# Eight projections of a two-block fp32 kernel computed as seven quarter products instead of eight

## The reference, cut to what matters

```python
# first block, x is (256, 1024)
yf = jnp.square(jax.nn.relu(hf @ w_up[l])) @ w_down[l]        # w_down (4096, 1024)
x = x + rmsnorm(yf, g_norm[l, 5])
# second block, h is (272, 1024): 16 meta tokens ahead of x
    return (y * g) @ w_o, v_first                             # time mixing, w_o (1024, 1024)
    return (jax.nn.silu(gate) * val) @ w_down                 # both FFNs, (2816, 1024)
            if layer == N_A:
                kvn = rms_norm(h, kv_norm_g)
                k_sh = to_padded_heads(kvn @ sb_wk)
                v_sh = to_padded_heads(kvn @ sb_wv)
            q = to_padded_heads(hn @ sb_wq[j])
            mix_out = stick_breaking_attention(q, k_sh, v_sh) @ sb_wo[j]
        h = h + mix_out
        h = h + conv_glu_ffn(rms_norm(h, norm_ffn_g[layer]), ffn_up[layer], ffn_conv_w[layer],
                             ffn_conv_b[layer], ffn_down[layer])
```

## Time and profile before

| | |
|---|---|
| median of 3 runs | 1638.88 us (1638.53 to 1639.74) |
| the profiled execution | 1636.88 us, of which its span is 1634.8 us |
| PE busy | 1536.2 us, 94% of the span |
| PEld busy | 1290.2 us, 79% |
| DVE busy | 527.2 us, 32% |
| ACT busy | 343.8 us, 21% |
| HBM read | 187.45 MB, 115 GB/s over the span |

### The profile page before, as it was taken

One profiled execution on the slowest core, in us unless ns is written; L12 is line 12 of the kernel. 1 busy time (PEld: TensorE's weight loads), 2 busy tenths in 40 slices (PEclk: granted clock), 3 DMA queues, 4 the chain that ended last, 5 costly groups with the idle time before them and its releaser, 6 DMA issues.

```text
span 1634.8 us, 25810 instructions
## 1 busy us (share of the span) xinstructions
PE 1536.2 (94%) x10548; PEld 1290.2 (79%) x10548; DVE 527.2 (32%) x977; ACT 343.8 (21%) x613; POOL 30.3 (2%) x47
## 2 busy tenths in 40 slices
PE   8999999989999879998888999999998879999997
PEld 6888788988888758577774888888886768888886
DVE  2140233331100273547535244431112542444301
ACT  1231103231100112200111223310102652323101
POOL 0130000000000000000000000000001100000000
PEclk9999999999999999899997999999999669999999
DMA  8444243354444304130000444444443003444441
GB/s 333 143 129 154 77 143 115 132 185 154 150 146 154 115 26 129 52 104 4 4 3 0 142 142 142 144 151 155 149 147 116 0 0 116 143 143 148 144 155 52
DMA packets 54435, 189.75 MB, mean 116 GB/s; under 512 B 6961, under 2 KB 9137, under 8 KB 53970
## 3 DMA queue, kind: packets, MB, share of 16 engines
q1 hardware_dynamic: 50480, 180.67, 33.3%
q10 hardware_dynamic: 3874, 7.85, 1.5%
HBM read 187.45 MB, written 1.05 MB: 115 GB/s over the span
## 4 chain that ended last, share of the span: by engine, by line
PE 89%; DVE 6%; issue 3%; ACT 1%; DMA 0%; POOL 0%; DVEq 0%; ACTq 0%; SPq 0%; PEldq 0%; POOLq 0%
PE ps L1365 88%; DVE arena L1165 1%; DVE arena L1193 0%; DVE arena L1302 0%; DMA ring<-in_stream 0%; DVE rs L1829 0%; DVE arena L1306 0%; DVE arena L1192 0%; DVE arena L1007 0%; DVE arena L999 0%; DVE res L1838 0%; DVE arena L997 0%; DVE arena L1846 0%; DVE arena L1315 0%; ACT L1648 0%
## 5 line engine op out<-in xcount | busy, mean ns | idle before, releaser
L1365 PE MATMUL ps<-arena,ring 128*128 128x272 f32 (+2 forms) x5504 | 1212.1, 383 | 19.7 <-DMA ring<-in_stream 8.2
L1365 PEld LDWEIGHTS ps<-arena,ring 128*128 128x128 f32 x5504 | 1028.3, 192 | 201.9 <-issue 16.0
L1365 PE MATMUL ps<-arena 64*64 64x64 f32 (+7 forms) x3828 | 177.8, 246 | 46.0 <-DVE arena L1315 12.2
L1365 PEld LDWEIGHTS ps<-arena 64*64 64x64 f32 (+3 forms) x3828 | 142.1, 141 | 80.8 <-issue 42.0
L1365 PE MATMUL ps<-arena,consts 128*128 128x16 f32 (+7 forms) x438 | 116.3, 425 | 19.9 <-DVE arena L1306 6.0
L1365 PEld LDWEIGHTS ps<-arena,consts 128*128 128x128 f32 (+3 forms) x438 | 84.8, 234 | 47.3 <-DVE arena L1306 6.1
L910 ACT ACTIVATE arena<-arena,cols 128x272 f32<-128x272 f32 x88 | 53.7, 613 | 184.5 <-DVE arena L1130 184.3
L1137 DVE SCALAR_TENSOR_TENSOR arena<-arena,cols 128x271 f32<-128x271 f32 (+1 forms) x176 | 84.1, 498 | 15.1 <-ACT arena L910 3.2
L1130 DVE TENSOR_TENSOR arena<-ps,rs 128x272 f32<-128x272 f32 x88 | 38.9, 442 | 149.5 <-PE ps L1365 147.7
L1079 DVE TENSOR_TENSOR res<-res,ps 128x272 f32<-128x272 f32 x32 | 14.0, 439 | 194.6 <-PE ps L1365 194.6
L891 ACT ACTIVATE arena<-res 128x272 f32<-128x272 f32 x32 | 13.8, 430 | 212.2 <-DVE res L1079 212.2
(11 more groups left out here) (219 smaller groups left out, 692.1 us busy)
## 6 DMA issues: line engine op xcount, KB each, us to landing
ring<-in_stream SPq DMA_DIRECT2D x342, 512.0 KB, 3.2
consts<-in_consts ACTq DMA_DIRECT2D x1, 1516.0 KB, 8.5
arena<-in_x_t ACTq DMA_DIRECT2D x1, 1024.0 KB, 5.8
arena<-in_mem_t ACTq DMA_DIRECT2D x1, 1024.0 KB, 4.8
res<-in_x_t ACTq DMA_DIRECT2D x1, 1024.0 KB, 14.2
out_t<-arena SPq DMA_DIRECT2D x4, 256.0 KB, 3.0
arena<-in_g ACTq DMA_DIRECT2D x1, 640.0 KB, 5.6
arena<-in_w ACTq DMA_DIRECT2D x2, 256.0 KB, 4.8
```

The lines of the kernel that those rows point to most:

```text
L1365: return nc.tensor.matmul(out, lhs, rhs, start=start, stop=stop)
```

## The change

Two neighbouring output tiles and two neighbouring input tiles make a 256x256 piece of the weights, cut in four quarters a11, a12, a21, a22; the tokens are cut in two halves (t = 128 of 256, or T2 = 136 of 272). The 2x2 product of quarters, which takes eight products of half width, is made from seven (Winograd's form of Strassen's algorithm), each with accumulation over the input tiles in PSUM:

- DVE makes four sums of the weight quarters (`weight_sums`, four instructions 128x512 for each pair of blocks, into one of two buffers) and four sums of the activations' quarters (`x_sums`).
- PE multiplies in the order 1, 6, 7, 4, 5, 2, 3 (`seven_products`); products 6, 7 and 3 and half of the operands come from the sums.
- ACT copies product 1 out of PSUM (`keep_first_product`), since an instruction then reads only one PSUM operand; DVE puts the seven products together into two output tiles (`quads_to_y`, `quads_to_res`, `quads_scaled`).

A pair of output tiles now has 28 matmuls for each group of four pairs of input tiles (21 for the last group of an FFN's down, which has three), where it had 64 wide ones per four blocks. `down` has 4 pairs of 4 groups; `ffa_down` and `ffb_down` 4 pairs of 3 groups (4, 4, 3); the square ones a single group per pair, with the first pair of tiles of `rw_o`, `sb_k` and `sb_o` left as it was. The PSUM banks of even and odd pairs alternate (0 to 3, 4 to 7), and PE starts pair i when the results of pair i - 2 have been taken. The activations' sums of the three down projections are made inside the loops of the up projections. SP's loads of the down projections come in pairs of blocks that belong together. Some one-use semaphores were merged (`arms_pe`, `arms_dve`) to free numbers.

```diff
+        ORDER = (1, 6, 7, 4, 5, 2, 3)
+        SPLIT = {1: (0, 0), 6: (0, 1), 7: (1, 0), 4: (1, 1), 5: (2, 0), 2: (2, 1), 3: (3, 0)}
+        WIDE = {7: (0, 0), 5: (0, 1), 4: (1, 0), 3: (1, 1), 1: (2, 0), 6: (2, 1), 2: (2, 2)}
...
+        def seven_products(pe, mm, name, second=None):
+            y = SEVEN[name]
...
+            x_of = {1: b11, 2: b21, 3: b22, 4: t4, 5: t1, 6: t2, 7: t3}
+            for i in range(y.i0, y.n):
+                if i >= 2:
+                    pe.wait_ge(ev[name], y.off + 2 * (i - 1))
+                if second and i == y.i0 + 1:
+                    second()
+                for g, n in enumerate(y.groups):
...
+                    w_of = {1: a11, 2: a12, 3: s4, 4: a22, 5: s1, 6: s2, 7: s3}
+                    arrived(pe, b)
+                    arrived(pe, b + 1)
...
+                    for p in ORDER:
+                        if p in (6, 7, 3):
+                            pe.wait_ge(w_summed, done + {6: 2, 7: 3, 3: 4}[p])
+                        for l in range(n):
+                            last = mm(product_at(y, i, p), w_of[p][:, l, :], x_of[p][:, 4 * g + l, :],
...
+                        if g == len(y.groups) - 1 and p in (6, 4, 2):
+                            last.then_inc(products, 1)
+                    last.then_inc(used, 2)
+
+        def weight_sums(dve, tt, name, i, g):
...
+            if b - 4 >= y.block(y.i0) or not y.own:
+                dve.wait_ge(used, b - 2)
+            tt(s1, a21, a22, ALU.add).then_inc(w_summed, 1)
+            dve.wait_ge(w_summed, done + 1)
+            tt(s2, s1, a11, ALU.subtract).then_inc(w_summed, 1)
+            tt(s3, a11, a21, ALU.subtract).then_inc(w_summed, 1)
+            dve.wait_ge(w_summed, done + 2)
+            tt(s4, a12, s2, ALU.subtract).then_inc(w_summed, 1)
+
+        def x_sums(link, tt, name, at=slice(None)):
...
+            link(tt(t1, b12, b11, ALU.subtract))
+            link(tt(t2, b22, t1, ALU.subtract))
+            tt(t3, b22, b12, ALU.subtract)
+            tt(t4, b21, t2, ALU.subtract).then_inc(x_summed, 1)
+
+        def seven_vector(dve, tt, name, quads, then=None):
...
+            for at, (_, i, g) in enumerate(work):
+                if at + 1 < len(work):
+                    weight_sums(dve, tt, *work[at + 1])
+                if g == 0 and at and at < len(work) - bool(then):
+                    quads(i - 1)
+            quads(y.n - 1)
...
-            tiles("rw_o", FIRST["rw_o"], 8, bb, L, norm=gated_slice)
+            tiles("rw_o", FIRST["rw_o"], 2, bb, L, norm=gated_slice)
+            seven_products(pe, mm, "rw_o")
...
+            def quads_to_res(name, i, which, queries=False):
...
+                dve.wait_ge(p1_kept, y.pair(i) + 1)
+                tt(u2, p1, pr(6), ALU.add)
+                link(tt(o[0], o[0], p1, ALU.add))
+                dve.wait_ge(products, 3 * y.pair(i) + 2)
+                tt(u3, u2, pr(7), ALU.add)
+                tt(o[1], o[1], u2, ALU.add)
+                link(tt(e[0], e[0], pr(4), ALU.add))
+                tt(e[0], e[0], u3, ALU.add)
+                link(tt(e[1], e[1], u3, ALU.add))
+                dve.wait_ge(products, 3 * y.pair(i) + 3)
+                tt(e[1], e[1], pr(5), ALU.add).then_inc(ev[name], 1)
+                link(tt(o[1], o[1], pr(5), ALU.add))
+                tt(o[0], o[0], pr(2), ALU.add)
+                if i:
+                    link(add_squares(2 * i))
+                dve.wait_ge(used, y.block(i + 1))
+                tt(o[1], o[1], pr(3), ALU.add).then_inc(ev[name], 1)
...
+            def quads_scaled(name, i, dst):
...
+                dve.wait_ge(used, y.block(i + 1))
+                dve.wait_ge(p1_kept, y.pair(i) + 1)
+                link(tt(u2, p1, product_at(y, i, 6), ALU.add))
+                tt(quarters[:, 2, :], p1, product_at(y, i, 2), ALU.add)
+                link(tt(uv, two(7), over(u2, 2), ALU.add))
+                tt(quarters[:, 0:4:3, :], uv, two(4), ALU.add)
+                link(tt(quarters[:, 1, :], uv[:, 0, :], product_at(y, i, 5), ALU.add))
+                part = dst[:, 2 * i:2 * i + 2, :]
+                tt(part, part, over(rs[:, 0:L], 2), ALU.mult).then_inc(ev[name], 2)
...
-            take_scaled("sb_v", 0, vT)
...
+            seven_vector(dve, tt, "sb_k", lambda i: quads_scaled("sb_k", i, kT), then="sb_v")
+            dve.wait_ge(hq_scaled, 1)
+            x_sums(link, tt, "sb_q")
+            seven_vector(dve, tt, "sb_v", lambda i: quads_scaled("sb_v", i, vT), then="sb_q")
...
-            pe.wait_ge(up_sq, GB + FF)
...
+            seven_products(pe, mm, "down")
```

More of the change, by code:

```diff
@@ L157, in wait, with block, pair, group @@
         eng.wait_ge(self.sem, self.at[name] + n)
+@dataclass
+class Seven:
+    first: int
+    t: int
+    groups: list
+    banks: tuple
+    place: dict
+    i0: int
+    n: int
+    off: int
+    own: bool
+    pair0: int = 0
+    group0: int = 0
+    sums0: int = 0
+    def block(self, i, g=0):
+        return self.first + 2 * (len(self.groups) * i + g)
+    def pair(self, i):
+        return self.pair0 + i - self.i0
+    def group(self, i, g):
+        return self.group0 + len(self.groups) * (i - self.i0) + g
 class Space:
```

378 lines of the change are left out of this document (264 added, 114 removed).

## The result

The changed kernel took 1599.26 us (median of four runs, 1594.21 to 1602.27), the kernel before 1639.31 us (1638.53 to 1642.63) beside it: a ratio of 0.9749, 95% interval 0.9719 to 0.9779, so 2.5% faster, 40 us by the medians. The forecast was 1598.5 us.

A forecast was written before the change was run, and what follows sets the result against it. PE, busy 94% of the span, was taken to bound the kernel; -43.6 + 0.8 + 0.4 + 2.0 + 0.65 - 0.8 = -40.5 us from 1636.9 gave 1596.4, plus 2.0 for the median: 1598.5, range 1591 to 1614.

The forecast's parts named there:

- The likeliest case: Whole kernel: the forecast with its small costs, 1592 to 1606 us, chance 0.68.
- Spacing, -43.6 us: PE in all eight changed projections: narrow instructions at 111.6 ns (128 columns) and 115.8 ns (136) save 43.6 us.
- the 118.3 kept for the range: 136-column instructions on PE: 118.3 ns each would cost 5.5 us more, giving 1604; counted within the 0.68 case.
- `down`: Sequence mixer's down projection: PE saves 10.5 us, the end costs 0.65 more, the start 0.8 less.
- FFN downs: `ffa_down` and `ffb_down`: PE saves 9.35 us each, 18.7 for both, with nothing added behind the last product.
- `rw_o`, `sb_o`: Both output projections: PE saves 2.55 us each but waits 0.1 for banks and 0.3 for `hf`, 0.8 for both.
- `sb_v`'s bank wait, 0.4 us: After `sb_k`: DVE needs 13.3 us, PE needs those banks after 13.0; a wait of 0.4 us.
- Stick attention, 2.0 us: Ahead of stick attention: 2.4 us behind the last matmul of `sb_q` instead of one 0.44 take; 2.0 us more.
- Rival "PE waits in the square stages": Square projections: 0.1 us more per DVE instruction makes pairs late, about 1614 us; chance 0.20 for 1606 to 1625.
- Rival "DVE becomes the bound": Square projections and FFN down projections: 0.3 us more per DVE instruction costs 65 us, giving 1663; chance 0.03.
- Rival "loads not hidden": All narrow products: a whole 140 ns weight load per instruction costs 78 us, giving 1677; chance 0.03.
- Clock: Stick attention's first bursts: some 3 us of PE idling ahead may lower the clock, 1 to 3 us, inside the range.

The follow-up runs named there:

- the halves: Kernel before, eight products kept but each matmul of the eight changed projections cut in two by columns; 1653.35 us, ratio 1.0101, and 1653.31 us, 1.0105, when repeated.
- the version that starts early: Changed kernel with stick attention's first unit no longer waiting for the last take of `sb_q`; 1593.85 us, ratio 0.9740 against the kernel before.

## Why the prediction was right

The likeliest case came true with its mechanism and its size: 1598.5 forecast, 1599.26 and 1597.74 measured, inside 1591 to 1614. That the median came within 1 us is luck: single executions span 1594 to 1603. The steps as measured give some -41.4 us and not -40.5: -43.3 of PE's work, and waits of +2.05 ahead of stick attention, +0.4 at the end of `down`, +0.4 at the end of the last FFN and -0.95 at the start of `down`. By its steps:

- **Spacing, -43.6 us.** Right. 111.6 ns at 128 columns from the row, and 115.8 at 136 from the line; the 118.3 kept for the range was not needed. The reason given (the longer of two things that overlap, not their sum) is what the run with fewer columns shows; that the other one is the load is likely and not shown by itself.
- **`down`.** -10.07 against -9.85: -10.45 of PE's work and +0.38 of waiting at the end, forecast at -10.5 and 0.65. PE's wait at its start went from 1.51 to 0.55 us, -0.96 against -0.8; the stretch's -1.15 has chance in it, as that start lay anywhere from 447.3 to 448.4 us in changed kernels.
- **FFN downs.** PE's busy time in the last FFN fell by 9.3 us (239.41 to 230.09), as forecast. The stretch fell by 8.93: "behind the last product nothing" was mis-sized by 0.4 us. PE's wait for the last total went from 0.95 to 1.34 us, since DVE had an addition and a sum of squares still to do: its last addition starts 0.64 us behind PE's end, where the take had started 0.11 behind.
- **`rw_o`, `sb_o`.** The waits of 0.4 us each did not come, by small margins. DVE follows PE by 0.3 us and not 0.5, so in `rw_o` the banks of pair 1 were free 6.2 us into pair 2 of 6.5. Slice 7 of `hf` was there 16.0 us behind the end of pair 1, and PE wanted it at 16.2. Undoing the two gave back 2.6 and 2.4 us, all of the 2.55.
- **`sb_v`'s bank wait, 0.4 us.** Not there either: in that stretch PE waited 3.14 us in all, and 3.15 is the wait ahead of stick attention.
- **Stick attention, 2.0 us.** Right: 3.15 against 1.10, and undone by starting the first unit early.
- **Rival "PE waits in the square stages".** Its condition, 0.1 us more per DVE instruction, did not hold (0.293 us for 136 columns). The row of 306 ns that spoke for it is the mean of two instructions, one of 166 and one of 445 ns. Its mechanism is real: with each weight sum doubled those stages were the first to give way.
- **Rival "DVE becomes the bound".** The doubled sums put the kernel 0.8% behind the kernel before, so DVE's margin is what the change lives on: 157 us more of DVE would have turned 40 us of gain into a loss of 14.
- **Rival "loads not hidden".** Excluded by the spacing, and the halves show no 140 ns.
- **Clock.** The mechanism is right: the first bursts of stick attention ran at the lower clock in all six profiles with the long idling and in none of the eight without. Its size was overrated: 0 to 1.3 us and not 1 to 3. Of the first profile's +2.28 us, 1.3 is this; the rest is the draw of the later clock.

## What to carry to other kernels

Trading one wide product in eight for narrower ones pays as long as the narrow one's columns still last as long as its weight load: read the spacing of an existing narrow stream and where the line through the wide ones crosses it, here 111.6 ns and some 131 columns. Compare the other engine's work with PE's pair by pair and not over the kernel: DVE at 48% of the span had room in `down` for twice its sums, and almost none in the square projections. And compare kernels by stretches cut at the same marks: those at full clock repeat to 0.01 us and show half a microsecond, while the medians carry 5 us of clock. Cut at the same instruction each time: one burst earlier is 1.8 us here.

## What was not expected of the hardware

- The granted clock's draw is the noise of this kernel. Of unaltered executions, time mixing took 332.1 to 339.0 us at 0.94 to 0.90, and stick attention 90.4 to 93.2 us at 0.69 to 0.63. One part of it has a cause in the program: 3.1 us of idling in place of 1.1 put the next 4 us at 0.50 to 0.70 in place of 1.00.
- Below some 131 columns fp32 instructions keep one pace, 111.6 ns at 96, 120 and 128 columns.
- When PE had to wait for DVE several times in a row (the doubled sums), the clock of a stage that was at 1.00 in every other run was 0.93. That is one profile.
- Weight sums that ran while GpSimd copied keys were slower, and so were the copies. In the timeline of DVE and POOL of the changed kernel, at `sb_v`, the sums last 0.78 and 0.89 us where their mean is 0.69, and the copy between them 0.88:

```profile
1205.96 0.78 DVE L705 TENSOR_TENSOR arena<-arena,ring 128x512 f32<-128x512 f32 x1
1206.14 0.88 POOL L1569 COPY arena<-arena 128x272 f32<-128x272 f32 x1
1206.66 0.89 DVE L706 TENSOR_TENSOR arena<-ring 128x512 f32<-128x512 f32 x1
```

  Alone such a copy took 0.42 us in the kernel before and in the version that starts early. It cost nothing here, as PE was covered.
